# The moves of the FFN's hidden values issued by ScalarE instead of SyncE

## What is computed

```
h2 = _rms_norm(x, norm_ffn)
gate, up = jnp.split(h2 @ w_gate_up, 2, axis=-1)      # FFN_HIDDEN = 2816
return x + (jax.nn.silu(gate) * up) @ w_down
```

## Time and profile before

| | us |
|---|---|
| device time, median of three runs | 799.5 (798.94 to 800.38) |
| profiled execution, device time | 799.06 |
| its span in the trace | 797.2 |
| PE busy in it | 791.5 |
| DVE / ACT busy in it | 570.7 / 404.6 |

### The profile page before, as it was taken

How to read it: one execution, slowest core, us unless ns; L and a number is a source line. 1 busy time by engine, 2 the same in 40 slices (tenths; PEclk the granted TensorE clock), 3 DMA queues, 4 the chain that set the end, 5 groups by cost and what they waited for, 6 DMA issues and landing times.

```text
span 797.2 us, 10273 instructions
## 1 busy us (share of the span) xinstructions
PE 791.5 (99%) x3792; PEld 650.2 (82%) x3792; DVE 570.7 (72%) x852; ACT 404.6 (51%) x541; POOL 67.9 (9%) x121
## 2 busy tenths in 40 slices
PE   8999999999999999999999999999999999999998
PEld 6888787878888888888888877887788888888886
DVE  7888988877585756656678778798675757656563
ACT  6865646554264443543476556465542644543431
POOL 5944000000000000000006100000000000000000
PEclk9999999999999999999999999999999999999999
DMA  8664536545466767676673625474446566675651
GB/s 306 200 195 140 169 134 226 192 148 180 133 226 186 228 215 219 194 225 190 187 254 116 228 83 185 141 255 159 159 159 199 169 209 206 232 226 183 215 183 53
DMA packets 112353, 149.64 MB, mean 188 GB/s; under 512 B 14248, under 2 KB 75440, under 8 KB 112304
## 3 DMA queue, kind: packets, MB, share of 16 engines
q1 hardware_dynamic: 112304, 148.98, 57.9%
HBM read 142.54 MB, written 1.05 MB: 180 GB/s over the span
## 4 chain that ended last, share of the span: by engine, by line
PE 95%; POOL 3%; DMA 1%; SPq 0%; DVE 0%; issue 0%; POOLq 0%; DVEq 0%
PE big L1695 20%; PE big L1699 19%; PE big L1698 19%; PE mix L1695 10%; PE mix L1699 10%; PE mix L1698 10%; PE mix L1739 1%; PE mix L1838 1%; PE mix L1763 1%; DMA pos_i<-in_positions 1%; PE mix L1751 1%; PE mix L1785 1%; PE mix L1820 1%; POOL logits L766 1%; POOL rstd L728 0%; POOL logits L768 0%
## 5 line engine op out<-in xcount | busy, mean ns | idle before, releaser
L859 ACT ACTIVATE w_hi<-w_raw 128x2048 fp32r<-128x2048 f32 (+2 forms) x140 | 254.8, 1826 | 174.5 <-DMA w_raw<-in_w_gate_up 89.9
L1183 DVE TENSOR_TENSOR w_lo<-w_raw,w_hi 128x2048 fp32r<-128x2048 f32 (+3 forms) x142 | 305.9, 2161 | 46.6 <-ACT w_hi L859 44.5
L1695 PE MATMUL big<-w_hi,act_hi 128*128 128x512 f32 (+2 forms) x476 | 184.3, 387 | 0.4 <-DVE w_lo L1183 0.4
L1699 PE MATMUL big<-w_hi,act_lo 128*128 128x512 f32 (+2 forms) x476 | 181.5, 381 | 0.0
L1698 PE MATMUL big<-w_lo,act_hi 128*128 128x512 f32 (+2 forms) x476 | 181.4, 381 | 0.0
L1695 PE MATMUL mix<-w_hi,act_hi 128*128 128x512 f32 x352 | 137.1, 390 | 0.0
L1699 PE MATMUL mix<-w_hi,act_lo 128*128 128x512 f32 x352 | 137.0, 389 | 0.0
L1698 PE MATMUL mix<-w_lo,act_hi 128*128 128x512 f32 x352 | 136.9, 389 | 0.0
L1695 PEld LDWEIGHTS big<-w_hi,act_hi 128*128 128x128 f32 x476 | 89.5, 188 | 19.5 <-issue 2.3
L1699 PEld LDWEIGHTS big<-w_hi,act_lo 128*128 128x128 f32 x476 | 89.5, 188 | 17.1
L1698 PEld LDWEIGHTS big<-w_lo,act_hi 128*128 128x128 f32 x476 | 89.6, 188 | 15.8
(11 more groups left out here) (216 smaller groups left out, 744.8 us busy)
## 6 DMA issues: line engine op xcount, KB each, us to landing
w_raw<-in_w_in SPq DMA_DIRECT2D x44, 1024.0 KB, 5.1
w_raw<-in_w_gate_up SPq DMA_DIRECT2D x88, 512.0 KB, 5.0
w_raw<-in_w_down SPq DMA_DIRECT2D x22, 1024.0 KB, 5.0
w_raw<-in_w_o SPq DMA_DIRECT2D x8, 1024.0 KB, 5.0
probs<-merged SPq DMA_DIRECT2D x160, 32.0 KB, 2.8
w_raw<-in_b_w_out SPq DMA_DIRECT2D x4, 1024.0 KB, 5.9
w_raw<-in_w_in SPq DMA_DIRECT2D x4, 512.0 KB, 3.7
w_raw<-in_a_w_out SPq DMA_DIRECT2D x4, 512.0 KB, 4.1
```

The costliest lines, as they stand in the source:

```text
L859: nc.scalar.activation(high(u)[:, a:b], arrived(u)[:, a:b], ACT.Copy).then_inc(hi_ready, 1)
L1183: nc.vector.tensor_tensor(low(u)[:, a:b], arrived(u)[:, a:b], high(u)[:, a:b].bitcast(F32), ALU.subtract).then_inc(lo_ready, 1)
L1695: ins = nc.tensor.matmul(dst[:, 0:w], xh, wh, start=first and n == 0, stop=False)
L1699: ins = nc.tensor.matmul(dst[:, 0:w], xl, wh, start=False, stop=end)
```

## The change

`move_pair` is taken out of SP's program and put into ACT's with the same waits, the same order and the same sixteen transfers. On SP the moves stood behind a load four slots ahead of PE; on ACT they are in the slots `MOVE_AT[j]` and `MOVE_AT[j] + 1` themselves, eight in each, behind the steps of the slot. SP keeps the loads and the stores of the result.

```
-            def move_pair(l, j, quarters):
-                if quarters[0] == 0:
-                    for f in pair_of(j):
-                        for tb in range(TB):
-                            sp.wait_ge(*mix_is_drained(l, "gu", f, tb))
-                    if j > 0:
-                        sp.wait_ge(*hid_turned.nth(l, TB * j))
-                for a in quarters:
-                    for b in range(QUARTERS):
-                        c0 = N * (j % 2) + P * b
-                        sp.dma_start(hid_by_value[quarter(b), :, a, :], merged[quarter(a), :, c0:c0 + P]
-                                     ).then_inc(hid_moved.sem, 16)
...
-                    for j in range(LAST):
-                        for half in range(2):
-                            if SLOT[u] == MOVE_AT[j] + RING - 1 + half:
-                                move_pair(l, j, range(2 * half, 2 * half + 2))
...
+            def move_pair(l, j, quarters):
+                if quarters[0] == 0:
+                    for f in pair_of(j):
+                        for tb in range(TB):
+                            act.wait_ge(*mix_is_drained(l, "gu", f, tb))
+                    if j > 0:
+                        act.wait_ge(*hid_turned.nth(l, TB * j))
+                for a in quarters:
+                    for b in range(QUARTERS):
+                        c0 = N * (j % 2) + P * b
+                        nc.scalar.dma_start(hid_by_value[quarter(b), :, a, :], merged[quarter(a), :, c0:c0 + P]
+                                     ).then_inc(hid_moved.sem, 16)
...
+                    for j in range(LAST):
+                        for half in range(2):
+                            if s == MOVE_AT[j] + half:
+                                move_pair(l, j, range(2 * half, 2 * half + 2))
```

## The result

The changed kernel takes 801.18 us (median of 20 runs, 799.90 to 803.26), the kernel before 798.88 us in the same series (797.96 to 800.78). The ratio is 1.0025, 95% interval 1.0019 to 1.0032: **slower by 2.0 us** (1.5 to 2.6; the medians by themselves lie 2.3 us apart). The forecast was slower by 3.9 us, from stops of TensorE (PE) at pairs 1 and 4; 801.18 us lies at the near end of its range of 801.2 to 807.6, just outside.

The account below looks back on a forecast made before the run. PE, busy in 791.5 of 797.2 us, was taken to bound the kernel. Stalls of 1.4 + 0.55 = 1.95 us per layer, 3.9 in all, on the profiled 799.06 gave 803.0, so 803.4 for the median; range 801.2 to 807.6.

Parts of the forecast that it names:

- PE bounds the FFN, nothing to win there: Both FFN stretches: PE busy 165.00 of 165.00 us, so fewer SP issues and earlier weights return at most 0.4 us.
- The issue runs under the pass, its price is SP's: ACT's second lump starts with the weight pass before it and runs under it; each issue costs 0.64 us.
- the dear issue: Rival: an ACT issue doesn't run under a pass (810.3 us) or takes 0.8 us (816.5 us); chance 0.20.
- The chain at pair 1: Layer 0, lumps through high part, tanhs, hidden steps, low parts, transposes: margins 0.9 and 0.2 us before PE's units 49, 50.
- Pair 4's margin of -0.1: At pair 4 DVE's last hidden step ends at 379.15, PE's transposes load 0.2 before 379.06: 0.1 us late.
- pairs 0, 2 and 3 covered: Low parts of these pairs still ready 2.0 to 2.9 us before PE needs them, so no stop there.
- landing covered: Pair 1's last move, issued at 278.9 with longest landing 4.8 us, arrives before DVE takes it up at 285.4.
- Both layers alike: Layer 1's FFN has the same order and length as layer 0's, so the 1.95 us stall counts twice.
- The collision term d: Extra time of sixteen ACT issues held by SP's weight issues: 1.6 us at pair 1, 0.45 at pair 4.
- That PE would stop at pair 1: PE stalls at pair 1 for about d - 0.2, 1.4 us per layer, d being the sixteen issues' extra time.
- covered after all: Rival: an ACT issue costs 0.64 us or less and nothing collides; 799.5 to 800 us, chance 0.31.

## Why the forecast was right in kind, in part by luck, and wrong in size

- *PE bounds the FFN, nothing to win there*: right. SP's lost issues and the earlier weights brought nothing that shows.
- *The issue runs under the pass, its price is SP's*: right. 0.02 us after the pass's start, 0.65 us per issue against 0.64. This rules out the dear issue.
- *The chain at pair 1*: right to 0.1 us. With this execution's late start of 1.7 us taken off, the first issue is at 268.71 (268.7 forecast), the lumps end at 274.62 and 279.82 (273.8 and 278.9), and the low part of unit 50 is ready at 291.50 - 1.7 = 289.8 (288.9). The whole lateness, 0.9 us, is that of the lumps, and 0.74 of it one issue of 1.36 us.
- *Pair 4's margin of -0.1; pairs 0, 2 and 3 covered; landing covered*: right, by the runs with some pairs on SP.
- *Both layers alike*: right in the stretches, not in the packets. A packet of q8 met a lump of pair 4 in layer 1 and not in layer 0, which makes 0.7 us.
- *The collision term d*: **the step that failed**. The forecast put 1.6 us at pair 1 and 0.45 at pair 4 for SP's load issues falling into ACT's lumps, as the middle between nothing and each of them waited for. The runs show nearly nothing of it (up to 0.1 us in a lump). In its place stand about 0.08 us per lump for the dearer spacing on ACT, 0.16 per pair, and what the forecast put at nothing without a word, that an issue can last longer than 0.6 us for reasons outside the two queues: beside an instruction packet by 0.2 to 1 us, and a gap of 0.3 us at one place. Together they make half of the 3.9 us. No row of before could size the term, as only SP issued there; its 5.07 us in most lumps, given under the rival that it was covered, tells of transfers in flight and not of a second queue that issues.
- *That PE would stop at pair 1*: **luck**. With the term at its measured size, 0.16 us per pair, the forecast's steps give no stop at pair 1 (margin 0.2) and 0.26 us at each pair 4, 0.5 us in all, which is its rival *covered after all*. The 0.64 and 0.53 us that PE lost at pair 1 came by the chain of the forecast, but from packets and a gap that were not in it.

The rule from the Trainium skill by which the result would have been 807.6 us (Perfetto Trace Analysis, DMA Instruction — HWDGE (DVE, Sync): one issue holds the descriptor generator and the next waits) does not show between SP and ACT here: 15.76 and 15.41 us side by side, 15.56 and 15.44 alone, so no queue waited out the other's issues. The long issues were in the trace of before too: SP has three in layer 1, the longest of 1.41 us. Rows 4 show 225 to 390 us alone, in which the longest took 0.72.

## What to carry to other kernels

Before transfers are moved to an engine that computes, work out for each place how much time lies between its next result and the engine that needs it, and split the issues so that no lump is longer than that: here eight, four and four cost nothing where eight and eight cost 2 us. Let the margin be over 1 us for each lump of issues, since here an issue took up to 1.7 us instead of 0.6, at places that moved when PE's program got longer. And look at the same place in every layer before taking one margin for both.

## What the runs showed of the hardware

- Issues of moves on SP and on ACT hardly slow each other (0.64 and 0.66 us with both at work). SP's load issues may be slowed a little: in the first FFN the longest took 0.72 us, against 0.52 in the kernel before. In the kernel with only transfers eight of them took 7.69 us, but the first four 0.45 to 0.52 each and only the later ones 0.9 to 1.7; no run has eight alone, so that this is ACT's doing is not shown.
- At a fixed count of its own instructions ACT's queue paused for 0.32 us between two issues, whatever PE's program was.
- An issue in progress when a 16 KB instruction packet of PE's queue is fetched takes 0.8 to 1.7 us in 34 of 37 cases, on either engine. The Trainium skill (Runtime: NRT & Kernel Launch, Instruction fetch mechanics) tells of refills in blocks of 256 instructions by a queue of the engine's own, whose cost is mostly hidden. The trace agrees on the block, and for PE on the hiding; the cost fell on another engine's issue. Through what the two meet was not tried.
- After waits of PE of 2.8 to 3.4 us (five times), the granted clock was 0.50 to 0.61 in the next 4 us, and PE slipped by 1.8 to 3.1 us more than it had waited. After 2.4 and 2.6 us of waiting in two pieces (longest 1.8 and 2.0, at pair 4 of the two kernels with longer lumps) it stayed at 1.00.
